# Decoder layer on one core: token-block sums of the first MLP matmul kept as float32 in the places of their low halves, and the weight sums of that matmul in another order

## The reference

```python
mix_out = jnp.einsum('bsd,de->bse', merged, w_out[l])
x = _layer_norm(DEEPNORM_ALPHA * x + mix_out, ln1_gain[l], ln1_bias[l])

h = jnp.square(jax.nn.relu(jnp.einsum('bsd,df->bsf', x, w_ff1[l])))
ff_out = jnp.einsum('bsf,fd->bsd', h, w_ff2[l])
x = _layer_norm(DEEPNORM_ALPHA * x + ff_out, ln2_gain[l], ln2_bias[l])
```

## Time and profile before

| | us |
|---|---|
| median of 3 runs | 1583.99 |
| the runs | 1580.01, 1583.99, 1586.74 |
| the profiled execution | 1582.09 |
| its span, first to last instruction | 1580.4 |
| mean granted TensorE clock of it | 0.979 |

### The profile page before, as it was taken

How to read it: one execution, slowest core, us unless ns; L and a number is a source line. 1 busy time by engine, 2 the same in 40 slices (tenths; PEclk the granted TensorE clock), 3 DMA queues, 4 the chain that set the end, 5 groups by cost and what they waited for, 6 DMA issues and landing times.

```text
span 1580.4 us, 19531 instructions
## 1 busy us (share of the span) xinstructions
PE 1482.8 (94%) x7088; PEld 1225.7 (78%) x7088; DVE 1100.3 (70%) x1448; ACT 667.0 (42%) x1028; POOL 344.4 (22%) x224
## 2 busy tenths in 40 slices
PE   8999999999988797999999977999999989999994
PEld 6788888877877676788777766888888877888883
DVE  3787887879876868554367787666664457668768
ACT  3454554556554555342022234444443434433342
POOL 2544444345422232111131170000000000000003
PEclk9999999999999999999999999999999999999997
DMA  5101111211110100011441224444442588645542
GB/s 170 54 27 54 54 46 62 78 53 41 54 41 14 40 14 27 27 54 41 167 166 68 93 80 154 153 147 147 151 162 103 195 311 304 212 136 199 195 164 106
DMA packets 111359, 172.39 MB, mean 109 GB/s; under 512 B 6064, under 2 KB 71600, under 8 KB 111152
## 3 DMA queue, kind: packets, MB, share of 16 engines
q1 hardware_dynamic: 111280, 171.33, 31.8%
HBM read 127.27 MB, written 44.04 MB: 108 GB/s over the span
## 4 chain that ended last, share of the span: by engine, by line
PE 64%; DVE 14%; issue 10%; DMA 6%; POOL 3%; ACT 2%; SPq 1%; POOLq 0%; DVEq 0%; ACTq 0%
PE p_proj L726 6%; PE p_proj L730 6%; PE p_proj L728 6%; PE p_z L1072 4%; PE p_z L1076 4%; PE p_z L1074 4%; PE p_tr L825 2%; DMA f_c<-w_ff 2%; PE p_av L839 2%; PE p_z L1096 2%; PE p_z L1094 2%; PE p_z L1095 2%; PE p_proj L1072 2%; PE p_proj L1074 2%; PE p_proj L1076 2%
## 5 line engine op out<-in xcount | busy, mean ns | idle before, releaser
L726 PE MATMUL p_proj<-xt_h,w_hi 128*128 128x512 f32 x640 | 255.5, 399 | 0.7 <-DVE xt_l L1539 0.7
L730 PE MATMUL p_proj<-xt_h,w_lo 128*128 128x512 f32 x640 | 254.8, 398 | 0.0
L728 PE MATMUL p_proj<-xt_l,w_hi 128*128 128x512 f32 x640 | 252.3, 394 | 0.0
L2169 POOL TENSOR_TENSOR w_lo<-w_raw,w_hi 128x1024 fp32r<-128x1024 f32 x48 | 121.1, 2522 | 249.7 <-DVE w_hi L1546 249.2
L730 PEld LDWEIGHTS p_proj<-xt_h,w_lo 128*128 128x128 f32 x640 | 121.5, 190 | 24.1
L2293 POOL TENSOR_TENSOR row_odd<-row_odd,gains 128x1024 f32<-128x1024 f32 x4 | 9.6, 2392 | 598.7 <-ACT row_odd L1531 598.7
L726 PEld LDWEIGHTS p_proj<-xt_h,w_hi 128*128 128x128 f32 x640 | 121.3, 189 | 22.9 <-issue 0.8
L728 PEld LDWEIGHTS p_proj<-xt_l,w_hi 128*128 128x128 f32 x640 | 121.3, 190 | 21.4
L1539 DVE TENSOR_TENSOR d_al<-f_a,d_ah 128x1024 fp32r<-128x1024 f32 x56 | 68.5, 1224 | 88.2 <-ACT d_ah L1441 87.9
L1441 ACT ACTIVATE d_ah<-f_a 128x1024 fp32r<-128x1024 f32 x56 | 59.2, 1058 | 144.0 <-PE p_av L1096 54.9
L1094 PE MATMUL p_z<-d_bh,d_ah 128*128 128x512 f32 x256 | 100.7, 393 | 4.4 <-DVE d_bl L1539 4.4
(11 more groups left out here) (281 smaller groups left out, 3623.5 us busy)
## 6 DMA issues: line engine op xcount, KB each, us to landing
f_a<-h_terms SPq DMA_DIRECT2D x56, 512.0 KB, 3.5
w_raw<-w_in SPq DMA_DIRECT2D x40, 512.0 KB, 3.9
h_terms<-c SPq DMA_DIRECT2D x40, 512.0 KB, 2.7
f_b<-w_ff SPq DMA_DIRECT2D x40, 512.0 KB, 4.7
r<-w_ff SPq DMA_DIRECT2D x32, 512.0 KB, 3.8
gate_rows<-gst SPq DMA_DIRECT2D x12, 512.0 KB, 5.0
y<-x SPq DMA_DIRECT2D x8, 512.0 KB, 8.7
wo_raw<-w_out SPq DMA_DIRECT2D x8, 512.0 KB, 8.6
```

Of the source, the lines that this page charges most:

```text
L726: pe.matmul(o, w_hi[n_slot][:, k, :], xt_h[:, k, cols], start=(k == 0), stop=False)
L728: pe.matmul(o, w_hi[n_slot][:, k, :], xt_l[:, k, cols], start=False, stop=False)
L730: mm = pe.matmul(o, w_lo[n_slot][:, k, :], xt_h[:, k, cols], start=False, stop=(k == KT - 1))
L2169: pool.tensor_tensor(w_lo[slot][:, :, :], w_raw[:, :, :], w_hi[slot][:, :, :].bitcast(F32), ALU.subtract).then_inc(wt_lo, 1)
```

## The change

1. T1, T2, T3 and T4 of each pair, and B22, are written as float32 into the tile (and the columns of that pair) where their low halves will stand: x_f for 5, 6 and 7, and the low columns of res for 4 and 3. T2 of the last pair alone has a tile of its own, t2_last. ScalarE makes one more copy per pair, that of B22 (`x22_f`).
2. The low halves of 6, 5, 3, 7 and 4 are no longer made pair by pair. `sums_low(m, first, end)` on VectorE makes those of several pairs in one instruction, in place: product 6 for pairs 0 to 2 after block 6's normalization and for pair 3 later; 5, 7, 4 and 3 for all four pairs during round 0. GpSimd makes no low halves of them.
3. T3 and T4 of the last pair, and the weight sums of products 7 and 3 of round 0, move from GpSimd to VectorE.
4. In all rounds the weight sums are s1 = r21 + r22 (in r_s1, product 5), s2 = s1 - r11 (in r11, product 6), s3 = r22 - s2 (in r21, product 7) and s4 = r12 - s2. The loads' conditions follow.
5. The orders of ScalarE and VectorE in round 0 are other ones: VectorE reads u3 and c22 before it begins on the weights of round 1.

The diff, cut to its core:

```diff
-for _m in (1, 2, 7, 5, 6, 4, 3):
+for _m in (1, 2, 5, 6, 7, 4, 3):
     HIGH_END[_m, 0] = len(HIGH_END) + 1
...
+        t2_last = at("t2_last", 219, [P, 4, P])
+        x_f = {m: at(f"x_f{m}", 72 + 16 * i, [P, 4, NH]) for m, i in ((6, 1), (5, 2), (7, 3))}
...
-        raw = {1: r11, 6: r11, 2: r12, 3: r12, 5: r21, 4: r22, 7: r_s3}
+        raw = {1: r11, 6: r11, 2: r12, 3: r12, 7: r21, 4: r22, 5: r_s1}
...
 load_21(n):
-                    sp.wait_ge(a_lo[5], n)
-                    sp.wait_ge(w_sum, 4 * n - 4 + 3)
+                    sp.wait_ge(a_lo[7], n)
 load_22(n):
                     sp.wait_ge(a_lo[4], n)
-                    sp.wait_ge(w_sum, 4 * n - 4 + 2)
+                    sp.wait_ge(w_sum, 4 * n - 1)
...
 wait_up(n, m), n == 0:
                     if m == 1:
                         pe.wait_ge(o_read, 2 * TB - 2)
-                        pe.wait_ge(x1_lo, 10)
+                        pe.wait_ge(x1_lo, 7)
                     elif m == 2:
-                        pe.wait_ge(x1_lo, 11)
+                        pe.wait_ge(x1_lo, 8)
                     elif m == 6:
                         pe.wait_ge(o_read, 2 * TB)
-                        pe.wait_ge(t12_lo, 7)
+                        pe.wait_ge(x_low_done, 2)
                     elif m == 5:
-                        pe.wait_ge(t12_lo, 8)
+                        pe.wait_ge(x_low_done, 3)
                         pe.wait_ge(t12_ready, 8)
-                        pe.wait_ge(x1_lo, 12)
-                    elif m in (7, 4):
-                        pe.wait_ge(t34_lo, {7: 7, 4: 8}[m])
+                        pe.wait_ge(x1_hi, 12)
+                    elif m in (7, 4, 3):
+                        pe.wait_ge(x_low_done, {7: 4, 4: 5, 3: 6}[m])
...
 x_high(tb), odd:
                     act.wait_ge(t12_ready, 2 * j + 2)
-                    act.activation(x_block(6, 0, j), t2_f[:, :, :], ACT.Copy).then_inc(t_hi, 1)
+                    act.activation(x_block(6, 0, j), x_sum(6, j), ACT.Copy).then_inc(t_hi, 1)
+                    act.activation(x_sum(3, j), by_block(p_proj[:, 1, :]), ACT.Copy).then_inc(x22_f, 1)
+                    act.activation(x_block(3, 0, j), by_block(p_proj[:, 1, :]), ACT.Copy).then_inc(x1_hi, 1)
                     act.wait_ge(t12_ready, 2 * j + 1)
-                    act.activation(x_block(5, 0, j), t1_f[:, :, :], ACT.Copy).then_inc(t_hi, 1)
-                    act.activation(x_block(3, 0, j), by_block(p_proj[:, 1, :]), ACT.Copy).then_inc(x1_hi, 1)
+                    act.activation(x_block(5, 0, j), x_sum(5, j), ACT.Copy).then_inc(t_hi, 1)
...
 ScalarE, round 0:
-            for m in (7, 5, 6):
-                a_high(m, 0)
+            a_high(5, 0)
+            a_high(6, 0)
             x_high(TB - 1)
             sums_high(3)
+            a_high(7, 0)
+            a_high(4, 0)
             square_first(0)
-            a_high(4, 0)
             a_high(3, 0)
...
 x_low(tb), odd:
-                dve.tensor_tensor(t2_f[:, :, :], by_block(p_proj[:, 1, :]), t1_f[:, :, :], ALU.subtract)\
+                dve.tensor_tensor(x_sum(6, j), by_block(p_proj[:, 1, :]), x_sum(5, j), ALU.subtract)\
                    .then_inc(t12_ready, 1)
-                for m, f in ((6, t2_f), (5, t1_f), (3, None)):
-                    if f is None:
-                        dve.wait_ge(x1_hi, 3 * j + 3)
-                        sub(x_block(3, 1, j), by_block(p_proj[:, 1, :]), x_block(3, 0, j)).then_inc(x1_lo, 1)
-                    else:
-                        dve.wait_ge(t_hi, 4 * j + {6: 1, 5: 2}[m])
-                        if m == 6:
-                            dve.wait_ge(t12_ready, 2 * j + 2)
-                        sub(x_block(m, 1, j), f[:, :, :], x_block(m, 0, j)).then_inc(t12_lo, 1)
+
+            def sums_low(m, first, end):
+
+                dve.wait_ge(t_hi, 4 * (end - 1) + {6: 1, 5: 2, 7: 3, 4: 4}[m] if m != 3 else 1)
+                if m == 3:
+                    dve.wait_ge(x1_hi, 12)
+                if m == 6:
+                    dve.wait_ge(t34_ready, 6)
+                low, whole, high = x_whole(m, first, end)
+                sub(low, whole, high).then_inc(x_low_done, 1)
...
             layer_norm1(TB - 2, 0, 64)
+            sums_low(6, 0, 3)
             layer_norm1(TB - 1, 1, 64, lambda: x_low(TB - 2))
             x_low(TB - 1)
...
+            def weights_s1(n):
+                dve.wait_ge(r21_in, 16 * (n + 1))
+                dve.wait_ge(r22_in, 16 * (n + 1))
+                dve.wait_ge(a_lo[5], n)
+                add(r_s1, r21, r22).then_inc(w_sum, 1)
+
+            def weights_s2(n):
+                dve.wait_ge(w_sum, 4 * n + 1)
+                dve.wait_ge(a_lo[1], n + 1)
+                minus(r11, r_s1, r11).then_inc(w_sum, 1)
+
             def weights_s3(n):
...
                 dve.wait_ge(w_sum, 4 * n + 2)
+                minus(r21, r22, r11).then_inc(w_sum, 1)
...
 VectorE, the rounds:
-            for m in (5, 7, 4):
-                a_low(m, 0)
+            sums_low(6, 3, 4)
+            sum_t3(3)
+            sum_t4(3)
+            sums_low(5, 0, 4)
+            a_low(5, 0)
+            weights_s3(0)
+            take_u2(0)
+            sums_low(7, 0, 4)
+            a_low(7, 0)
+            sums_low(4, 0, 4)
+            a_low(4, 0)
+            weights_s4(0)
+            take_u3(0)
+            take_c22(0)
+            a_low(3, 0)
+            sums_low(3, 0, 4)
             for n in range(ITERS):
                 after = n + 1 < ITERS
                 if n == 0:
-                    take_u2(0)
-                    a_low(3, 0)
+                    a_low(1, 1)
+                    take_c21(0)
+                    weights_s1(1)
+                    weights_s2(1)
                     weights_s3(1)
-                    weights_s1(1)
-                    a_low(1, 1)
-                    weights_s2(1)
                 else:
                     take_c12(n - 1)
                     a_low(3, n)
                     if after:
-                        weights_s3(n + 1)
                         weights_s1(n + 1)
                     hidden_s1(n - 1)
                     hidden_s3(n - 1)
                     if after:
                         a_low(1, n + 1)
                         weights_s2(n + 1)
+                        weights_s3(n + 1)
                     take_u2(n)
                     hidden_s2(n - 1)
                     hidden_s4(n - 1)
                 if after:
                     a_low(6, n + 1)
                     a_low(5, n + 1)
-                    take_u3(n)
-                    take_c22(n)
+                    if n:
+                        take_u3(n)
+                        take_c22(n)
                     a_low(7, n + 1)
                     a_low(2, n + 1)
                     weights_s4(n + 1)
-                    take_c21(n)
+                    if n:
+                        take_c21(n)
                     a_low(4, n + 1)
...
 GpSimd, sums(j) and round 0:
-                pool.tensor_tensor(b11_f[:, :, :], t2_f[:, :, :], b11_f[:, :, :], ALU.subtract).then_inc(t34_ready, 1)
-                pool.tensor_tensor(b21_f[:, :, :], b21_f[:, :, :], t2_f[:, :, :], ALU.subtract).then_inc(t34_ready, 1)
-                for i, (m, f) in enumerate(((7, b11_f), (4, b21_f))):
...
+                pool.tensor_tensor(x_sum(7, j), x_sum(6, j), b11_f[:, :, :], ALU.subtract).then_inc(t34_ready, 1)
+                pool.tensor_tensor(x_sum(4, j), b21_f[:, :, :], x_sum(6, j), ALU.subtract).then_inc(t34_ready, 1)
...
-            sums(3)
-            pool.wait_ge(w_sum, 3)
-            pool.wait_ge(a_lo[2], 1)
-            pool.tensor_tensor(r12[:, :, :], r12[:, :, :], r11[:, :, :], ALU.subtract).then_inc(w_sum, 1)
```

More of the change, by code:

```diff
@@ L264, in layer_kernel @@
         xh[2], xl[2] = at("x_h2", 168, [P, 4, NH], F32R), at("x_l2", 207, [P, 4, NH], F32R)
-        b11_f, b21_f, t1_f, t2_f = (at(n, 215 + 2 * i, [P, 4, P])
-                                    for i, n in enumerate(("b11_f", "b21_f", "t1_f", "t2_f")))
+        b11_f, b21_f = (at(n, 215 + 2 * i, [P, 4, P]) for i, n in enumerate(("b11_f", "b21_f")))
+        t2_last = at("t2_last", 219, [P, 4, P])
+        x_f = {m: at(f"x_f{m}", 72 + 16 * i, [P, 4, NH]) for m, i in ((6, 1), (5, 2), (7, 3))}
         A_AT = {1: 176, 2: 0, 6: 8, 5: 16, 7: 24, 4: 48, 3: 56}
@@ L269, in layer_kernel @@
         al = {m: at(f"a_l{m}", o + 4, [P, 4, 256], F32R) for m, o in A_AT.items()}
-        r11, r12, r21, r22, r_s3 = (at(n, o, [P, 4, 256]) for n, o in
-                                    (("r11", 200), ("r12", 32), ("r21", 36), ("r22", 40), ("r_s3", 44)))
-        raw = {1: r11, 6: r11, 2: r12, 3: r12, 5: r21, 4: r22, 7: r_s3}
+        r11, r12, r21, r22, r_s1 = (at(n, o, [P, 4, 256]) for n, o in
+                                    (("r11", 200), ("r12", 32), ("r21", 36), ("r22", 40), ("r_s1", 44)))
+        raw = {1: r11, 6: r11, 2: r12, 3: r12, 7: r21, 4: r22, 5: r_s1}
         p1, u2, c11, c21, c12, c22, s1h, s3h = (at(n, o, [P, 2, NH]) for n, o in
```

(44 more changed lines are left out.)

36 lines of the change are left out of this document (17 added, 19 removed).

## The result

The changed kernel took 1567.13 us in the median (1564.35 to 1568.19, 4 runs) beside 1585.37 for the kernel before on the same chip: a ratio of 0.9887 with a 95% interval of 0.9857 to 0.9917. The forecast was 1566.

The account below looks back on a forecast made before the run. TensorE bounds the kernel, busy 94% of the span, so gains must come from its pauses or clock before the last six rounds. 23.7 us gained by round 1, less 4.5 and 1.2, gives 18.0: 1584.0 to 1566, range 1559 to 1575.

Parts of the forecast that it names:

- Step 1: Output projection: pauses before normalized token blocks go, 11.93 us per block; block 6 turned 13.2 us earlier, product 1 14.2 earlier.
- rival (b): GpSimd and whole-block operations slow VectorE, as when both meet in block 6's normalization; 10 to 14 us gained, 1572; chance 0.17.
- Step 2: Block 7 and products 1, 2, 6: block 7's pause falls from 2.70 to about 1.8 us; product 6 starts 15.1 earlier.
- Step 3: Round 0's end: the 7.94 us pause before product 4 shrinks to about 1.5; round 1 starts 23.7 us earlier.
- Step 4: Round 1: VectorE's backlog makes u2 late, a new 4.5 us pause before product 7 plus 1.2 of clock; 18.0 gained.
- the wait for r22: Round 1, VectorE: about 2.3 us waiting for round 2's r22, issued after a_low(4) and landing 4.4 us later.
- Both sides start at u3: Round 1's pause, counted from u3: VectorE needs 33.0 us to u2, TensorE 28.6 to product 7, whatever came before.
- rival (a): Round 1's backlog is shorter if ScalarE and r22 are not late: pause 1 us, 22 to 23 gained, 1561; chance 0.12.
- The clock term: Slow clock after round 1's new pause costs 1.2 us, with 0 and 2.2 kept for the range.
- Step 5: Rounds 2 to 7 and the rest: no gain or loss, as u2 keeps 4 us of room in each round.
- (c): The projection doesn't speed up because something else is as late as VectorE; 3.8 us less a little gained, 1580; chance 0.08.
- (d): Slower: s1 waits for r22 in every round and u2 is late, deciding from a 9 us landing; 1592 and above; chance 0.03.

Follow-up runs that it names:

- the second execution: The changed kernel again, unedited, on the same chip as three of the edited kernels; 1567.14 us.
- s1 behind the hidden sums: Changed kernel with round 2's weight sum s1 moved behind the two hidden sums in round 1; 1566.63 us, ratio 0.9885 to the kernel before.
- the runs with a shorter low 3: Changed kernel with low halves made right after t2 for pairs 0 to 2 (1575.72 us), or in VectorE's idle time for pairs 0 and 1 (1570.59 us).
- the weight sums alone: Kernel before with only the order of the weight sums (and their loads' conditions) as in the change; 1586.39 us, ratio 1.0007 to the kernel before.
- the old order: Changed kernel with VectorE's order in round 0 as before: u3, c22 and c21 behind round 1's first weight sums and low halves; 1572.97 us, ratio 0.9917.

## Why the prediction was right, point by point

**Step 1, projection: right.** Blocks 1 to 5 are turned 11.8 us apart and block 6 9.05 after block 5, without a pause, at a clock of 1.00. Block 6 gained 13.8 (13.2 predicted; the 11.93 per block was 0.15 too long). The forecast pause before product 1 came, at 0.52 instead of 1.2. The meeting of rival (b) came too, in the order that spared the row. VectorE's and GpSimd's timelines after block 5:

```profile
903.28 1.29 DVE L1879 SCALAR_TENSOR_TENSOR rows<-rows,vecs,gains 128x1024 f32<-128x1024 f32 x1
904.48 3.94 DVE L1556 TENSOR_TENSOR x_l<-x_f,x_h 128x1536 fp32r<-128x1536 f32 x1
```

```profile
903.65 3.16 POOL L2300 TENSOR_TENSOR a_l<-r,a_h 128x1024 fp32r<-128x1024 f32 x1 [2.50 <-ACT a_h L1417]
```

L1879 began 0.37 us before GpSimd's a_low(1) and kept its 1.29 us, whereas in the earlier trace rows GpSimd was 0.10 ahead and it took 3.33. Now a_low(1) waited (3.16 instead of 2.34) and then held up the joined low 6, which took 3.94. That is 2.1 us more than the 1.8 that the prediction gave low 6 by itself, and the pause before product 1 stayed at 0.52 all the same. The Trainium skill (SBUF — State Buffer, Who interferes with whom) has the engine that issues first keep the shared port while the other waits; both orders are shown here, and the trace agrees.

**Step 2: right.** Block 7's pause was 1.50 (1.8 predicted), and GpSimd's instructions still cost its normalization time:

```profile
911.53 2.39 POOL L2309 TENSOR_TENSOR r_s<-r,r 128x1024 f32<-128x1024 f32 x1
914.00 3.26 POOL L2312 TENSOR_TENSOR r<-r_s,r 128x1024 f32<-128x1024 f32 x1
```

```profile
912.36 2.64 DVE L1867 SCALAR_TENSOR_TENSOR rows<-rows,vecs,gains 128x1024 f32<-128x1024 f32 x1
915.11 2.17 DVE L1873 SCALAR_TENSOR_TENSOR vecs<-vecs 128x1 f32<-128x1 f32 x1
```

In block 6's normalization, without GpSimd beside them, the same two lines took 1.27 and 0.22 us: even an instruction of one element per partition stood until GpSimd's was over.

**Step 3: right.** Product 4's pause was 1.41 (1.5). The VectorE sequence with whole-block subtractions of 2.28 us held, and low 3 and a_low(7) were in time. Round 1 started 24.8 us earlier (23.7).

**Step 4: the mechanism was right; two of its terms were too small, and one part of the count isn't on the path.** The pause came at product 7 of round 1, for u2, at 5.64 us (6.06 in the second execution) where 4.5 stood. The mis-sized term is the wait for r22: I took a landing of 4.4 us from the earlier trace rows; in the changed kernel the loads of that line landed in 5.1 in the median and 6.9 at most, and VectorE waited:

```profile
DMA to landing us min/median/max: 3.9/5.1/6.9
```

```profile
965.87 1.23 DVE L1949 TENSOR_TENSOR r_s<-r,r 128x1024 f32<-128x1024 f32 x1 [3.22 <-issue]
```

That is 3.2 instead of 2.3 us, 0.9 of the 1.1 by which the pause was longer. The bracket names no releaser; that it is the load follows from its issue at 960.41, some 5.5 us earlier, and from the run with s1 behind the hidden sums. "Both sides start at u3" holds, but the count treats all the work behind u3 as VectorE's backlog, and its first part isn't: the runs with a shorter low 3 put c21 at the same 7.09 us behind u3, at the end of product 4. So rival (a) couldn't have come from less work ahead of c21, only from the two waits that it names: they came, with 1.39 for ScalarE and 3.22 for r22, and without them the pause would have been 1.0 (an estimate, 5.64 less both).
The clock term was too small as well. Round 1 took 952.25 to 998.07 = 45.82, less 38.08 and 5.64: 2.1 us, and 3.1 by the same count in the second execution, where 1.2 stood with 2.2 as the upper end. The windows of the changed kernel after the pause:

```profile
974.00:978.00 4.00, 3.63 (x9) 2.89 (x10) 3.97 (x5) 0.00 (x0) 0.00 (x0) 0.50 0.47 186
978.00:982.00 4.00, 4.00 (x19) 3.27 (x18) 0.94 (x2) 0.05 (x1) 0.00 (x0) 0.96 0.19 76
```

The clock stood at 0.50, the 1.2 GHz level, for 4 us after 5.6 us of rest. The guess of a cost between that of 2.70 and that of 6.89 us of pause had no row of its own length behind it. In all step 4 cost 7.7 us instead of 5.7, and the 1.1 gained more in steps 1 to 3 paid half of it back: 17.0 instead of 18.0.

**Step 5: right.** Rounds of 38.08 us without a pause, in the changed kernel and with the weight sums alone.

**The other rivals.** (c) fell with step 1. (d) fell with the weight sums alone, where no later round had a pause; the longest landing of that line was 6.9 us in the changed kernel's first profile and 7.7 in its second, against the 9 from which it would decide.

## What to carry to other kernels

Joining small instructions and moving them behind the critical part pays where they were ahead of something late, but their work goes somewhere: follow the engine's order behind the new place, instruction by instruction, until it has idle time again, and look there for what the bounding engine asks of it. Within such a backlog it is the order that counts: one read of a PSUM bank taken six instructions earlier gave 8.9 us, half of what the whole change had given, while shortening work ahead of a wait for TensorE itself gave nothing. Put what the bounding engine waits for ahead of what waits for a load.

## What the runs showed of the hardware

- Even a pause of 3.68 us (s1 behind the hidden sums) was followed by slow matmuls: round 1 took 43.48 there, 1.7 more than 38.08 and the pause. By the same count the pauses of 5.64, 5.85, 5.89 and 6.06 us cost 2.1, 2.3, 2.2 and 3.1 on top, a third to a half of themselves. Longer ones didn't cost in proportion: counted from product 4 to round 1, against two products of 5.44, the 7.94 of the kernel before cost 1.9 and the 11.82 of the old order 2.7.
- Shorter pauses may cost or not. Block 7's 1.50 us was followed by a granted clock of 1.00 (the window from 909 to 952). The pause of 2.33 before block 7 left the clock at 1.00 in one kernel and was followed by 0.57 in another, with the same work around it, and cost 1.6 us there; of the two pauses of 2.2 us in the earlier trace rows one was followed by a block 1.5 us longer.
- Two profiles of the same kernel were 3.6 us apart at block 1 (849.24 and 852.86), and the time between block 1 and round 2 differed by 1.6. So the interval of one profile shows effects of 3 us and more; smaller ones are shown here by the wait itself, in the engine's rows.
